# Two attention layers on one core: the sliding-window outputs gathered by fours into a whole PSUM bank

## The reference, cut to what matters

```python
def swa_sink_attention(q, k, v, sink, mask):     # q: 8 heads, k and v: 2 heads, 64 features each
    ...
    s = jnp.einsum('bnqhgd,bnkhd->bnhgqk', qb, kb).astype(jnp.float32) * scale
    s = jnp.where(mask[None, :, None, None, :, :], s, -jnp.inf)
    m = jnp.maximum(jnp.max(s, axis=-1, keepdims=True), sk)
    e = jnp.exp(s - m)
    p = e / (jnp.sum(e, axis=-1, keepdims=True) + jnp.exp(sk - m))
    o = jnp.einsum('bnhgqk,bnkhd->bnqhgd', p.astype(v.dtype), vb)
    return o.reshape(B, S, SWA_WIDTH)

def hybrid_mixer(...):
    ...
    return jnp.concatenate([y_diff, y_swa], axis=-1) @ w_out
```

## Time and profile before

| | |
|---|---|
| median of 3 runs | 1314.74 us (1314.21 to 1315.25) |
| the profiled execution, its own time | 1314.84 us |
| its span, first to last instruction | 1313.0 us |
| around the span | 1.84 us |
| TensorE clock granted, mean | 0.998 of full speed |
| PE / weight load busy | 99% / 84% |
| DVE / ACT / POOL busy | 70% / 49% / 5% |
| mixers' attention steps | about 577 to 645 us and 1046 to 1114 us |

### The profile page before, as it was taken

One profiled execution on the slowest core, in us unless ns is written; L12 is line 12 of the kernel. 1 busy time (PEld: TensorE's weight loads), 2 busy tenths in 40 slices (PEclk: granted clock), 3 DMA queues, 4 the chain that ended last, 5 costly groups with the idle time before them and its releaser, 6 DMA issues.

```text
span 1313.0 us, 17226 instructions
## 1 busy us (share of the span) xinstructions
PE 1303.2 (99%) x6977; PEld 1102.6 (84%) x6977; DVE 925.0 (70%) x1190; ACT 641.0 (49%) x839; POOL 67.4 (5%) x145
## 2 busy tenths in 40 slices
PE   9999999999999999999999999999999999999997
PEld 7887788888888888887888888888888878888886
DVE  5798767766547666788876666776666888676665
ACT  7777645343344444357554444444443576543441
POOL 3121000000000000000300000000000003000000
PEclk9999999999999999999999999999999999999999
DMA  9643466555555555553565555565555444755550
GB/s 297 207 154 106 122 239 193 193 192 192 191 198 190 192 192 193 192 150 108 183 205 191 192 192 193 166 236 190 188 188 187 161 129 131 241 188 190 188 185 33
DMA packets 155311, 238.11 MB, mean 181 GB/s; under 512 B 4264, under 2 KB 110784, under 8 KB 155232
## 3 DMA queue, kind: packets, MB, share of 16 engines
q1 hardware_dynamic: 154576, 235.95, 54.8%
q0 software_dynamic: 384, 0.54, 0.3%
q10 hardware_dynamic: 272, 0.52, 0.1%
HBM read 235.95 MB, written 1.05 MB: 180 GB/s over the span
## 4 chain that ended last, share of the span: by engine, by line
issue 86%; PE 9%; POOL 2%; POOLq 1%; DVE 1%; ACT 1%; DVEq 0%; DMA 0%; SPq 0%
PE ps L1603 2%; PE ps L1604 2%; PE ps L1605 2%; POOL drs L574 1%; POOLq L573 1%; PE ps L1673 1%; POOL lrs L574 1%; PE ps L1756 0%; DMA xres<-in_x_dram 0%; PE ps L1765 0%; ACT ebuf L754 0%; PE ps L1780 0%; PE ps L1734 0%; DVEq L1094 0%; DVE ebuf L1112 0%
## 5 line engine op out<-in xcount | busy, mean ns | idle before, releaser
L543 DVE TENSOR_TENSOR wlo<-raw,whi 128x2048 fp32r<-128x2048 f32 x172 | 391.8, 2287 | 129.3 <-ACT whi L535 129.1
L535 ACT ACTIVATE whi<-raw 128x2048 fp32r<-128x2048 f32 x197 | 369.7, 1905 | 22.9 <-DMA raw<-in_w_up_dram 11.3
L1977 PE MATMUL ps<-xt_both,whi 128*128 128x512 f32 x1504 | 358.7, 390 | 0.0
L1977 PEld LDWEIGHTS ps<-xt_both,whi 128*128 128x128 f32 x1504 | 279.1, 188 | 55.9
L1982 PEld LDWEIGHTS ps<-xt_both,wlo 128*128 128x128 f32 x1504 | 193.4, 191 | 7.6
L1271 DVE TENSOR_REDUCE hid_a<-ps 128x512 f32<-128x1024 f32 (+1 forms) x98 | 115.3, 1177 | 119.0 <-PE ps L1982 119.0
L1982 PE MATMUL ps<-xt_both,wlo 128*128 128x256 f32 x1504 | 195.7, 283 | 0.0
L1603 PE MATMUL ps<-whi,ht_hi 128*128 128x512 f32 x480 | 187.7, 391 | 0.0
L1604 PE MATMUL ps<-wlo,ht_hi 128*128 128x512 f32 x480 | 187.3, 390 | 0.0
L1605 PE MATMUL ps<-whi,ht_lo 128*128 128x512 f32 x480 | 186.8, 389 | 0.0
L899 ACT ACTIVATE hid_b<-hid_a 128x512 f32<-128x512 f32 x40 | 25.2, 630 | 236.5 <-DVE hid_a L1271 236.5
(11 more groups left out here) (232 smaller groups left out, 1333.9 us busy)
## 6 DMA issues: line engine op xcount, KB each, us to landing
raw<-in_ffn_w_in_dram SPq DMA_DIRECT2D x80, 1024.0 KB
raw<-in_ffn_w_out_dram SPq DMA_DIRECT2D x44, 1024.0 KB
raw<-in_w_in_dram SPq DMA_DIRECT2D x36, 1024.0 KB
raw<-in_w_up_dram SPq DMA_DIRECT2D x16, 1024.0 KB
raw<-in_w_down_dram SPq DMA_DIRECT2D x16, 1024.0 KB
raw<-in_w_out_dram SPq DMA_DIRECT2D x8, 1024.0 KB
raw<-in_ffn_w_in_dram SPq DMA_DIRECT2D x16, 512.0 KB
raw<-in_w_out_dram SPq DMA_DIRECT2D x8, 512.0 KB
```

Of the source, the lines that this page charges most:

```text
L535: act.activation(whi[j][:, :], raw[j][:, :], ACT.Copy).then_inc(hi_done, 1)
L543: dve.tensor_tensor(wlo[j][:, :], raw[j][:, :], whi[j][:, :].bitcast(F32), ALU.subtract).then_inc(lo_done, 1)
L1977: pe.matmul(o(k).rearrange("p (j n) -> p j n", j=2), whi[w][:, block(b, k)], xt_both[:, :, b, :], start=b == 0, stop=False)
```

## The change

The outputs of the sliding units are made by fours, at two steps in place of four: units 0 to 3 at step 6 and units 4 to 7 at step 11. They fill all 512 columns of bank 7. ACT's high part and DVE's low part are then one instruction of 128x512 for four units, where they were one of 128x256 for two. Because four turned units must be held at once, units 2, 3, 6 and 7 go to `maps` (columns 0, 2, 4, 6) and units 0, 1, 4, 5 to the two buffers as before. The number of matmuls is the same.

```diff
-WINDOW_OUTS = {4: 0, 6: 2, 8: 4, 11: 6}
+WINDOW_OUTS, OUT_UNITS = {6: 0, 11: 4}, 4
...
+        def sliding_pt(f):
+            if f % 4 < 2:
+                return ptb2[f % 2][:, :]
+            c = 4 * (f // 4) + 2 * (f % 2)
+            return maps[:, c:c + 2, :].rearrange("p c n -> p (c n)")
...
-                act.activation(ptb2[f % 2][:, :], turned2(f), ACT.Copy).then_inc(pt_out, 1)
+                act.activation(sliding_pt(f), turned2(f), ACT.Copy).then_inc(pt_out, 1)
...
-            act.wait_ge(o_ready, UNITS * (l + 1) + f + 2)
-            act.activation(ot_hi[:, 4 + f // 2, :], ps[:, 7, 0:TOK], ACT.Copy).then_inc(o_act, 2)
+            act.wait_ge(o_ready, UNITS * (l + 1) + f + OUT_UNITS)
+            act.activation(ot_hi[:, 4 + f // 2:6 + f // 2, :], ps[:, 7, :].rearrange("p (k n) -> p k n", n=TOK),
+                           ACT.Copy).then_inc(o_act, OUT_UNITS)
...
-            dve.wait_ge(o_act, UNITS * l + f + 2)
-            dve.tensor_tensor(ot_lo[:, 4 + f // 2, :], ps[:, 7, 0:TOK], ot_hi[:, 4 + f // 2, :].bitcast(F32),
-                              ALU.subtract).then_inc(o_out, 2)
+            dve.wait_ge(o_act, UNITS * l + f + OUT_UNITS)
+            rows = slice(4 + f // 2, 6 + f // 2)
+            dve.tensor_tensor(ot_lo[:, rows, :], ps[:, 7, :].rearrange("p (k n) -> p k n", n=TOK),
+                              ot_hi[:, rows, :].bitcast(F32), ALU.subtract).then_inc(o_out, OUT_UNITS)
...
-            elif f % 2 == 0:
+            elif f % (OUT_UNITS if f < HALF else 2) == 0:
...
-                        m = pe.matmul(ps[r * HD:(r + 1) * HD, 7, f % 2 * P:(f % 2 + 1) * P], proj2[:, k, SV2 + r * HD:SV2 + (r + 1) * HD],
+                        m = pe.matmul(ps[r * HD:(r + 1) * HD, 7, f % 4 * P:(f % 4 + 1) * P], proj2[:, k, SV2 + r * HD:SV2 + (r + 1) * HD],
...
-                        layer_outputs(pe, l, WINDOW_OUTS[i])
-                        layer_outputs(pe, l, WINDOW_OUTS[i] + 1)
+                        for j in range(OUT_UNITS):
+                            layer_outputs(pe, l, WINDOW_OUTS[i] + j)
```

More of the change, by code:

```diff
@@ L1900, in layer_outputs @@
                 pe.wait_ge(v_read, 4 * l + 4)
-            pt = ptb2[f % 2] if f < HALF else maps[:, f - HALF, :]
+            pt = sliding_pt(f) if f < HALF else maps[:, f - HALF, :]
             for k in range(TT):
```

## The result

The changed kernel takes 1318.12 us (median of 20 runs, 1317.0 to 1319.6), the kernel before in the same comparison 1315.16 us (20 runs, 1314.2 to 1316.9): a ratio of 1.0019, 95% interval 1.0013 to 1.0025. By the bound of 0.2% this is no change, with the whole interval on the slow side; 1316.8 with a ratio of 1.0016 was forecast. The runs of either kernel fall into two clusters some 2 us apart (before: 11 near 1314.7 and 9 near 1316.7; after: 10 near 1317.2 and 10 near 1319.1), and within a cluster the difference is 2.4 us. The three runs shown before the prediction all lay in the lower one, and the range of 1314.8 to 1317.9 was laid around it: the lower cluster of the changed kernel lies inside, its median over all runs 0.2 us above. Runs e10 and e11 ask where the clusters come from.

What follows compares the result with a forecast made beforehand. PE, busy for 99% of the span, was taken to bound the kernel. A wait of +0.17 us at step 8 and +0.86 at step 11 made +1.03 a layer, +2.06 in two: 1316.8 us, range 1314.8 to 1317.9.

Steps and rivals of the forecast that it cites:

- A group of four costs 1.88 us, two cost 1.02.: PE's time for the outputs of four units in one group, 1.88 us, and of two units, 1.02 us.
- Step 4's gain is used up at step 6, by the maximum of unit 5.: Step 4 loses 1.02 us; at step 6 added work and a wait for DVE's maximum leave the tile 0.05 later.
- The turns of step 8 fall into two fours that wait for the divisions, +0.17.: At step 8 PE waits for DVE's divisions of units 6 and 7 and a split block: +0.17 us a layer.
- ACT costs nothing.: ACT's wider copies at step 6 cost nothing, since the exponentials of unit 6 behind follow 1.03 us of idle time.
- At 631.67 DVE waits for POOL, and the 0.26 end there.: Behind step 11, DVE's extra 0.26 us from its wider low part was to end in a wait for POOL.
- The rival "slower": Behind step 11 DVE falls behind and PE waits at unit 15's score: 1317.8 us, or 1318.4; chance 0.16.
- The pure gain: Rival: no new wait in the mixers, as the drain rule gives; -0.46 us a layer, 1313.8 us; chance 0.06.
- The sum: +0.17 at step 8 and +0.86 at step 11: +1.03 us a layer, +2.06 in two.
- "I am wrong if ...": Three signs: step 8's turns go without a gap, the second layer does otherwise than the first, PE waits behind step 11.

Runs made afterwards that it cites:

- e10: The kernel before, with three idle transposes on PE in the hole ahead of the second half of the first turned input: 1315.28 us, ratio 0.9999.
- e11: The changed kernel, with three idle transposes on PE in the hole ahead of the second half of the first turned input: 1317.77 us, ratio 1.0017.
- e4: The changed kernel with one needless DVE addition of 128x256 ahead of the divisions of units 6 and 7 at step 6: 1317.69 us, ratio 1.0020.
- e5: The kernel before with one needless DVE addition of 128x256 ahead of the divisions of units 6 and 7 at step 6: 1316.81 us, ratio 1.0010.
- e3: The changed kernel with DVE's low part of units 0 to 3 moved behind the divisions and the two split blocks: 1317.28 us, ratio 1.0018.
- e1: The changed kernel, but only units 0 to 3 by four at step 6; 4 and 5 at step 8, 6 and 7 at step 11: 1315.09 us.
- e9: The kernel before regrouped: units 0 and 1 at step 4, 2 to 5 at step 8, 6 and 7 at step 11: 1316.60 us, ratio 1.0010.
- e6: The changed kernel with DVE's low part of units 4 to 7 cut to two columns, ACT writing the outputs in its place: 1318.56 us, ratio 1.0019.
- e2: The changed kernel, but units 0 and 1 at step 4, 2 and 3 at step 6, only 4 to 7 by four: 1316.97 us, ratio 1.0016.
- e7: e1 with DVE's low part of step 6 moved behind the divisions and split blocks: 1323.70 us, ratio 1.0064.
- e8: The kernel before with DVE's low part of step 6 moved behind the divisions and split blocks: 1323.49 us, ratio 1.0062.

## Why the prediction was right, and where it was not

- *A group of four costs 1.88 us, two cost 1.02.* Right: 1.90 at step 6, 1.89 at step 11, and there 0.87 more than before (0.86).
- *Step 4's gain is used up at step 6, by the maximum of unit 5.* Right: the scores wait for it, and the tile was 0.07 later (0.05) in the first layer, 0.06 earlier in the second.
- *The turns of step 8 fall into two fours that wait for the divisions, +0.17.* The mechanism is right, by the trace (0.35 us of the weight load between the fours) and by e4 and e5. The size was +0.06 and -0.06: the low part's 0.26 delays the second division by 0.14 only, because the wait for ACT's exponentials between the two went away. Freeing DVE further (e3) runs into ACT's copy of the keys after another 0.14, a neighbour that I had listed (`qk_out`) and not priced.
- *ACT costs nothing.* Right: the exponentials still wait 0.91 us for DVE.
- *"At 631.67 DVE waits for POOL, and the 0.26 end there."* This is the step that failed. The waits for POOL move along with DVE. The 0.26 reach the heads' low part undiminished, where PE had 0.25 in hand: by themselves they cost about 0.1 us (second layer). With 0.28 more from a gap of DVE's, which no row before announced, PE loses 0.45 us in the first layer.
- *The rival "slower"* had the right engine (DVE gets later than PE beyond step 11) and the wrong place: the scores of step 15 went on time (33.65 - 24.74 = 8.91 us behind the scores of step 11, 8.90 before).
- *The pure gain* did not occur. By the Trainium skill, "TensorEngine Tiling (Array Packing)", Key Properties, a change of tiling mode drains PE; the page names no size. In the trace four units in one group take 1.90 us, two groups of two 2.04. Whether that difference is the drain no run shows, and in e1, e9 and the change it was lost again in a wait right behind.
- *The sum*: +1.03 a layer was forecast, +1.47 and +1.05 measured; the second layer is right by luck, by errors that cancel: step 8 less by 0.23, step 11 more by 0.06 and what lies behind more by 0.19.
- *"I am wrong if ..."* Of the three signs that the prediction names, two came: the second layer does otherwise than the first, and PE shows a wait behind step 11. The total held all the same, since what lies behind step 11 (0.70 us in two layers) and the lower loss at step 8 (0.34 us less) partly cancel.

What stays open: the gap at L1199 (there in the first layer of the change, e3, e6 and e11, one like it in e5, none in e4), and DVE's later start at step 4 of the second layer in e1, e2, e7 and e9. Both are up to 0.43 us, appear and vanish with edits elsewhere, and are of the size of the effects asked for here.

## What to carry to other kernels

On an engine that is full, work is not only a cost: it also covers the chain of the engines beside it. Before taking it away, note for the instruction behind it when its operands are ready; what it can gain is that distance and no more, and the work is still to be paid where it goes. And follow a delay of a side engine to the next place where the main engine needs it, however far off: it ends in slack only if that slack is idle time which the delayed instruction doesn't itself cause, and a wait for a third engine that started on the first one's result is not that.

## What the runs showed that I had not expected

- Two clusters of run times 2 us apart, which go with PE's pace in the first 11 us: 2.34 or 1.25 us for ten transposes.
- Of four waits of PE of 2.7 to 2.9 us (e7, e8), two were followed by 3 to 4 us mostly at a granted clock of 0.50 to 0.58, two by none.
- The tile that DVE released at 642.01 was followed by the next one at 642.35, after 0.34 us instead of 0.23, so this wait cost 0.1 us beyond itself.
- Gaps of up to 0.43 us on DVE in which it waits for nothing that is recorded: at the same instruction in the profiles of the change, e3, e6 and e11, at another in e5, and none in e1, e2, e7 and e9.
